# Latent attention scores from split operands, with the rotary parts stacked and the steps in another order

## The reference, cut to what matters

```python
c_q = rms_norm(h @ w_dq, cq_norm)
q = (c_q @ w_uq).reshape(b, s, MLA_HEADS, MLA_QK_NOPE + MLA_QK_ROPE)
q_nope = rms_norm(q[..., :MLA_QK_NOPE], q_nope_norm)
q_pe = rotary(rms_norm(q[..., MLA_QK_NOPE:], q_pe_norm), pos)
...
sc = (jnp.einsum('bqhd,bkhd->bhqk', qn, k_nope)
      + jnp.einsum('bqhr,bkr->bhqk', qp, k_pe)).astype(jnp.float32) * scale
sc = jnp.where(causal_mask(i, s), sc, NEG_INF)
a = jax.nn.softmax(sc, axis=-1)
return jnp.einsum('bhqk,bkhv->bqhv', a.astype(v.dtype), v)
```

## Time and profile before

| what | us |
|---|---|
| median of 3 runs | 2226.89 (2221.76 to 2227.26) |
| profiled execution | 2226.47 |
| its span, first to last instruction | 2224.7 |
| PE busy in the span | 2183.1 (98%) |
| DVE / ACT / POOL busy | 1276.9 (57%) / 945.7 (43%) / 804.4 (36%) |
| first scores of steps 1, 2, 3 | 763.40, 792.26, 824.28 |
| first scores of steps 7, 8 | 952.51, 984.93 |

### The profile page before, as it was taken

One profiled execution on the slowest core, in us unless ns is written; L12 is line 12 of the kernel. 1 busy time (PEld: TensorE's weight loads), 2 busy tenths in 40 slices (PEclk: granted clock), 3 DMA queues, 4 the chain that ended last, 5 costly groups with the idle time before them and its releaser, 6 DMA issues.

```text
span 2224.7 us, 25927 instructions
## 1 busy us (share of the span) xinstructions
PE 2183.1 (98%) x10008; PEld 1711.2 (77%) x10008; DVE 1276.9 (57%) x2198; ACT 945.7 (43%) x1558; POOL 804.4 (36%) x315
## 2 busy tenths in 40 slices
PE   8999999999999999999999999999999999999998
PEld 5777788888887767667888888887774688888887
DVE  6887665553258688773665562176967643333224
ACT  6676443333233566663344332233237532222224
POOL 1232444444443222113444444433330144444432
PEclk9999999999999999999999999999999999999999
...
DMA packets 58650, 199.97 MB, mean 90 GB/s; under 512 B 6720, under 2 KB 10320, under 8 KB 58528
## 3 DMA queue, kind: packets, MB, share of 16 engines
...
...
## 4 chain that ended last, share of the span: by engine, by line
PE 88%; DVE 7%; ACT 2%; issue 1%; DMA 1%; POOL 0%; SPq 0%; DVEq 0%; ACTq 0%
PE lin L535 24%; PE lin L537 24%; PE lin L536 24%; PE obank L869 1%; PE scores L847 1%; PE turn L668 1%; PE scores L851 1%; PE stat L674 1%; PE scores L1070 1%; PE lin L586 1%; PE obank L748 1%; PE lin L588 1%; PE lin L587 1%; PE scores L705 1%; PE obank L1046 1%
## 5 line engine op out<-in xcount | busy, mean ns | idle before, releaser
L2540 POOL TENSOR_TENSOR w_lo<-slots,w_hi 128x1024 fp32r<-128x1024 f32 (+4 forms) x309 | 801.5, 2596 | 1395.9 <-ACT w_hi L2021 1395.9
L2021 ACT ACTIVATE w_hi<-slots 128x1024 fp32r<-128x1024 f32 (+4 forms) x312 | 347.0, 1113 | 576.9 <-DMA slots<-in_w_ffn_in 281.0
L535 PE MATMUL lin<-g_hi,w_hi 128*128 128x512 f32 x1400 | 550.0, 393 | 0.0
L537 PE MATMUL lin<-g_hi,w_lo 128*128 128x512 f32 x1400 | 545.0, 389 | 0.0
L536 PE MATMUL lin<-g_lo,w_hi 128*128 128x512 f32 x1400 | 544.9, 389 | 0.0
L535 PEld LDWEIGHTS lin<-g_hi,w_hi 128*128 128x128 f32 x1400 | 262.8, 188 | 59.3 <-issue 5.0
L536 PEld LDWEIGHTS lin<-g_lo,w_hi 128*128 128x128 f32 x1400 | 262.8, 188 | 55.8 <-issue 1.7
L537 PEld LDWEIGHTS lin<-g_hi,w_lo 128*128 128x128 f32 x1400 | 262.7, 188 | 54.7
L1255 DVE TENSOR_TENSOR h<-lin,h 128x512 f32<-128x512 f32 x72 | 49.7, 690 | 306.1 <-PE lin L537 296.9
L536 PE MATMUL lin<-f_lo,w_hi 128*128 128x512 f32 x528 | 205.4, 389 | 0.0
L535 PE MATMUL lin<-f_hi,w_hi 128*128 128x512 f32 x528 | 205.4, 389 | 0.0
...
## 6 DMA issues: line engine op xcount, KB each, us to landing
...
slots<-in_w_b_pair SPq DMA_DIRECT2D x8, 768.0 KB, 4.2
...
```

Source lines behind the costliest of these rows:

```text
L535: pe.matmul(bank[:, parity, :], hi, x_hi, start=k == 0, stop=False)
L537: mm = pe.matmul(bank[:, parity, :], lo, x_hi, start=False, stop=k == len(rhs) - 1)
L2021: ac.activation(w_hi[:, slot, at_], slots[:, slot, at_], ACT.Copy).then_inc(q.hi_made, 1)
L2540: po.tensor_tensor(w_lo[:, slot, at_], slots[:, slot, at_], w_hi[:, slot, at_].bitcast(F32), ALU.subtract).then_inc(q.weights_split, 1)
```

## The change

Queries and keys are split into hi and lo parts of type fp32r. A head's scores are now five passes for each query block: q_hi·k_hi, q_hi·k_lo, q_lo·k_hi (L852 to L854 of the changed kernel), and two for the rotary part. For these, `b_qp[:, x]` stacks the hi and the lo part of head x's rotary query on the 128 partitions, against the hi part of the rotary key, which fills both halves, and its lo part (L855, L856). ScalarE makes the hi parts (`high_`, `rope_highs`, once `rope_key_high`), VectorE the lo parts (`low_`, `rope_lows`, once `rope_key_low`). Keys and stacked rotary queries have a single set of buffers, so their hi parts wait until all scores of the step are done; the scores of step s wait for all splits of step s-1 (`qk_split`). A reciprocal now serves both heads. The transposed weights of k = 3 go to a free third of the bank, so `turn_(3)` follows `turn_(2)` without a wait. `straight`, which was in `roped`, has a place of its own. The orders of all three engines' steps are new. Copies of the products out of PSUM (`output`) stay on VectorE.

```diff
@@ -130,6 +130,10 @@
...
+B_QK = 2 * AH + 1
+B_QK_ORDER = {0: 1, 1: 2, 3: 3, 4: 4, 2: 6}
...
@@ -294,11 +298,11 @@
...
-        b_kp = area(at, S); at += S
+        b_kp, b_kp_hi, b_kp_lo = area(at, S), area_r("b_kp_hi", 22 * S, S), area_r("b_kp_lo", at, S); at += S
...
-        b_qn = area(at, 2, 2, S); at += 4 * S
-        b_kn = area(at, 2, 2, S); at += 4 * S
-        b_qp = area(at, 2, S); at += 2 * S
+        b_q = [(area_r(f"b_q_hi{y}", o, 2, S), area_r(f"b_q_lo{y}", o + 2 * S, 2, S)) for y, o in enumerate((12 * S, at))]; at += 4 * S
+        b_k = area_r("b_k_hi", at, 2, S), area_r("b_k_lo", at + 2 * S, 2, S); at += 4 * S
+        b_qp = area_r("b_qp", at, 2, S); at += 2 * S
...
@@ -839,25 +843,27 @@
...
                         if k == 0:
-                            pe.wait_ge(q.b_normed, 5 * s)
-                            pe.wait_ge(q.b_rope, s)
-                        wait(pe, q.b_biased, 8 * (s - 1) + 2 * k)
-                        qb = slice(i * P, (i + 1) * P)
+                            pe.wait_ge(q.qk_split, B_QK + 6 * s)
+                        qb, keys = slice(i * P, (i + 1) * P), slice(0, LEN[i])
+                        (q_hi, q_lo), (k_hi, k_lo) = b_q[1 - par], b_k
                         for x in range(2):
-                            pe.matmul(scores[:, x, 0:LEN[i]], b_qn[:, 1 - par, x, qb], b_kn[:, 1 - par, x, 0:LEN[i]],
-                                      start=True, stop=False)
-                        for x in range(2):
-                            rows = slice(64 * x, 64 * x + 64)
-                            pe.matmul(scores[:, x, 0:LEN[i]], b_qp[rows, 1 - par, qb], b_kp[rows, 0:LEN[i]],
-                                      start=False, stop=True).then_inc(q.b_scored, 1)
+                            wait(pe, q.b_biased, 8 * (s - 1) + 2 * k - 1 + x)
+                            to = scores[:, x, keys]
+                            pe.matmul(to, q_hi[:, x, qb], k_hi[:, x, keys], start=True, stop=False)
+                            pe.matmul(to, q_hi[:, x, qb], k_lo[:, x, keys], start=False, stop=False)
+                            pe.matmul(to, q_lo[:, x, qb], k_hi[:, x, keys], start=False, stop=False)
+                            pe.matmul(to, b_qp[:, x, qb], b_kp_hi[:, keys], start=False, stop=False)
+                            pe.matmul(to, b_qp[:, x, qb], b_kp_lo[:, keys], start=False, stop=True).then_inc(q.b_scored, 1)
...
                         for x in range(2):
                             n, i = 8 * pair + 2 * k + x, NQ - 1 - k
                             pe.wait_ge(q.b_weights, n + 1)
-                            wait(pe, q.b_tcopied, n - 1)
-                            turn_weights(b_sc[:, x, i, :], i, turn[:, x, :]).then_inc(q.b_turned, 1)
+                            if k < 3:
+                                wait(pe, q.b_tcopied, n - 1)
+                            to = turn[:, x, 2 * P:] if k == 3 else turn[:, x, :]
+                            turn_weights(b_sc[:, x, i, :], i, to).then_inc(q.b_turned, 1)
...
 
                 if not proj and attn:
-                    early(0); turn_(2, s - 2, late); score(0); turn_(3, s - 2, late); product(0); score(1); product(1); early(1); score(2)
+                    early(0); turn_(2, s - 2, late); turn_(3, s - 2, late); score(0); product(0); score(1); product(1); early(1); score(2)
...
                 lin_(0)
                 if s == 1:
-                    rotated_(0); sums(4, 0)
-                lin_(1); turn_(2, s - 2, late); score(0); lin_(2); lin_(3); sums(0)
-                turn_(3, s - 2, late); score(1); lin_(4); sums(1); product(0); score(2); sums(2); lin_(5)
-                product(1); turn_(0); sums(3); lin_(6); score(3); rotated_(); sums(4); turn_(1)
+                    rotated_(0); sums(4, 0); lin_(1); lin_(2); score(0); lin_(3)
+                else:
+                    lin_(1); turn_(2, s - 2, late); turn_(3, s - 2, late); score(0); lin_(2); lin_(3)
+                sums(0); score(1); lin_(4); sums(1); product(0); sums(2); score(2); lin_(5)
+                product(1); turn_(0); sums(3); score(3); lin_(6); sums(4); rotated_(); turn_(1)
...
@@ -1657,17 +1664,18 @@
...
-                            ve.wait_ge(q.b_exped, n + 1)
-                            ve.reciprocal(d, d).then_inc(q.b_recip, 1)
-                            ve.wait_ge(q.b_recip, n + 1)
+                            if x == 0:
+                                both = den[:, 0:8].rearrange("p (x i) -> p x i", x=2)[:, :, i]
+                                ve.wait_ge(q.b_exped, n + 2)
+                                ve.reciprocal(both, both).then_inc(q.b_recip, 1)
+                                ve.wait_ge(q.b_recip, 4 * (s - 1) + k + 1)
                             ve.tensor_scalar(b_sc[:, x, i, 0:LEN[i]], b_sc[:, x, i, 0:LEN[i]], d, None, ALU.mult)\
                                 .then_inc(q.b_weights, 1)
...
                 def normed(j):
...
-                        dst = (b_qn[:, par, 0, :], b_qn[:, par, 1, :], b_rt[:, 0, :], b_kn[:, par, 0, :],
-                               b_kn[:, par, 1, :])[j]
+                        dst = b_rt[:, 0, :] if j == 2 else b_ri[:, j, :]
...
+                def low_(j):
+                    if proj:
+                        hi, lo = b_q[par] if j < 2 else b_k
+                        x = j % 2 if j < 2 else j - 3
+                        ve.wait_ge(q.qk_rounded, B_QK + 6 * s + B_QK_ORDER[j])
+                        ve.tensor_tensor(lo[:, x, :], b_ri[:, j, :], hi[:, x, :].bitcast(F32), ALU.subtract).then_inc(q.qk_split, 1)
+
+                def rope_lows():
+                    ve.wait_ge(q.qk_rounded, B_QK + 6 * s + 6)
+                    for x in range(2):
+                        rows, other = slice(64 * x, 64 * x + 64), slice(64 - 64 * x, 128 - 64 * x)
+                        ve.tensor_tensor(b_qp[other, x, :], b_rt[rows, 1, :], b_qp[rows, x, :].bitcast(F32), ALU.subtract)\
+                            .then_inc(q.qk_split, 1)
+
+                def rope_key_low():
+                    ve.wait_ge(q.qk_rounded, B_QK)
+                    ve.tensor_tensor(b_kp_lo[:, :], b_kp, b_kp_hi[:, :].bitcast(F32), ALU.subtract).then_inc(q.qk_split, 1)
...
+                def straight():
+                    ve.wait_ge(q.b_normed, 5 * s + 3)
+                    ve.tensor_tensor(b_rt[:, 2, :], b_rt[:, 0, :], cosb[:, :], ALU.mult).then_inc(q.b_terms, 1)
+
                 def roped():
                     ve.wait_ge(q.b_rotated, s + 2)
                     ve.tensor_tensor(b_rt[:, 1, :], obank[:, :], sinb[:, :], ALU.mult).then_inc(q.b_terms, 1)
-                    ve.tensor_tensor(b_rt[:, 2, :], b_rt[:, 0, :], cosb[:, :], ALU.mult).then_inc(q.b_terms, 1)
                     ve.wait_ge(q.b_terms, 3 + 2 * s + 2)
-                    ve.tensor_tensor(b_qp[:, par, :], b_rt[:, 1, :], b_rt[:, 2, :], ALU.add).then_inc(q.b_rope, 1)
+                    ve.tensor_tensor(b_rt[:, 1, :], b_rt[:, 1, :], b_rt[:, 2, :], ALU.add).then_inc(q.b_rope, 1)
...
                 if s == 0:
-                    take_(0); take_(1); square_split(0); take_(2); square_split(1); take_(3); square_split(2); normed(0)
-                    take_(4); square_split(3); normed(1); take_(5); square_split(4); normed(2); take_(6); normed(3)
-                    roped(); normed(4)
+                    take_(0); take_(1); square_split(0); rope_key_low(); take_(2); square_split(1); take_(3); square_split(2); normed(0)
+                    take_(4); square_split(3); normed(1); take_(5); square_split(4); normed(2); low_(0); take_(6); normed(3); low_(1)
+                    straight(); low_(3); roped(); normed(4); low_(4); rope_lows()
                     return
-                take_(0); take_(1); biased(0); square_split(0); take_(2); square_split(1); take_(3); weights_(0)
-                normed(0); biased(1); take_(4); square_split(2); first_half(0); output(0); first_half(1); biased(2)
-                square_split(3); normed(1); weights_(1); first_half(2, 3); take_(5); normed(2); output(1); square_split(4)
-                take_(6); first_half(4, 5); roped(); weights_(2); first_half(6, 7); biased(3); normed(3); normed(4)
-                weights_(3)
+                take_(0); square_split(0); take_(1); biased(0); square_split(1); take_(2); weights_(0)
+                take_(3); square_split(2); biased(1); normed(0); take_(4); square_split(3); normed(1); low_(0); output(0); first_half(0, 1)
+                biased(2); low_(1); weights_(1); first_half(2, 3); take_(5); square_split(4); normed(2); output(1); straight()
+                first_half(4, 5); biased(3); normed(3); take_(6); weights_(2); first_half(6, 7); low_(3); roped(); normed(4)
+                weights_(3); low_(4); rope_lows()
...
@@ -2293,12 +2322,32 @@
...
-                            ac.wait_ge(q.b_turned, 8 * pair + 2 * k + x + 1)
+                            ac.wait_ge(q.b_turned, 8 * pair + 2 * (3 if k > 1 else k) + x + 1)
                             if k == 0:
```

(35 more changed lines are left out.)

## The result

The changed kernel took 2259.99 us (median of 4 runs, 2255.34 to 2262.67), the kernel before 2226.69 on the same chip (4 runs): ratio 1.015, 95% interval 1.0136 to 1.0163. It is slower by 33 us, where 11 were forecast, and the time lies outside the range of 2217 to 2247. The direction and the place were right; two sizes and the clock were not. The nearest rival, the third (2246 us), fell short as well. Of a later kernel (e10) one execution of ten took 4398.88 us; it is left out of that kernel's ratio, and nothing here explains it.

A forecast was written before the change was run, and what follows sets the result against it. The prediction took VectorE, with ScalarE in its chain, as the new bound. Start +8.3, steps 2 to 6 +2.2, step 7 +2.8 and step 8 -1.6 gave 2226.5 + 11.7 = 2238.2 us, range 2217 to 2247.

The forecast's parts named there:

- TensorE alone: In a steady step, TensorE without waits for other engines would need 30.0 us, after savings of 1.5, 0.2 and 0.4.
- VectorE's work: In a steady step, VectorE's real work: 21.4 us before, plus 2.8 for subtractions less reciprocals, 24.2 us.
- The two GpSimd blocks: In each steady step, VectorE stands beside GpSimd's subtractions: 2.8 us at straight, 2.3 at normed(4), 5.1 in all.
- one of the signs named for being wrong: In the changed profile, the forecast is wrong if VectorE's long instructions are others than straight and normed(4), and shorter.
- VectorE's waits: In a steady step, VectorE's idle waits by the new order, with hand-overs, sum to 3.4 us.
- the layout: VectorE's steady step laid out by the new order, dense from normed(1) to the end: 32.5 us against 32.09.
- Rival 3: In steady steps, TensorE idle 2 to 3 us gets a lower clock: step 33.7, total 2246 us; chance 0.12.
- The start: Up to the first scores of step 2: lin_(2) of step 1 waits 4.6 us for take_(0); +8.3 us.
- Step 7: Step 7: 4.8 us more of output subtractions, 2.3 less for one GpSimd instruction; 35.2 instead of 32.42, +2.8.
- step 8: Step 8, without projection: TensorE bounds it and keeps the savings, -1.6 us.
- Rivals 1 and 2: The second: in steady steps one of the two GpSimd blocks falls on harmless instructions, step 31, total 2228 us; chance 0.24.
- rival 1: In steady steps TensorE stays the bound, GpSimd meeting PSUM copies and waits: 2211 us; chance 0.14 together with another rival.

The follow-up runs named there:

- e10: The kernel before, with both weight splits on ScalarE moved to the beginning of the step and square_split(0), (1) behind take_(2): 2222.82 us, ratio 0.9988.
- e3: The changed kernel with GpSimd's subtraction for these steps' weights cut to 32 columns, TensorE reading hi parts instead, passes unchanged: 2222.32 us in one run.
- e8: The changed kernel with both weight splits on ScalarE moved to the beginning of the step, square_split(0), (1) behind take_(2): 2219.9 us, ratio 0.9972.
- e2: The changed kernel with take_(5) moved behind square_split(4) and normed(2) in VectorE's order: 2246.05 us in one run.
- e1: The changed kernel with discarded products on TensorE ahead of score(0) and of lin_(2) of step 1: 2246.54 us in one run.

## Why the prediction was wrong

**TensorE alone, 30.0 a step: right.** e3 shows 29.86 and e8 30.15 (the 1.5 for `scores` mixes two ways of counting, see above; from start to start they went from 7.7 to 6.4, 1.3). Its passes of 512, 384 and 256 columns went every 0.23, 0.17 and 0.12 us, and of 128 columns every 0.11 (0.12 taken).

**VectorE's work, 24.2: right.** 29.22 less 2.66 and 2.15 of blocks is 24.4, and e8 has 24.43.

**The two GpSimd blocks, 5.1: right in size** (4.8), but the first was placed wrongly: `square_split(4)` stood, not `straight`, which is one of the signs named for being wrong.

**VectorE's waits, 3.4: the first term that was mis-sized.** They are 34.52 - 29.22 = 5.3 us at full clock. Each wait that the layout lists came within 0.3 us: 1.22 before `square_split(0)` (1.2 forecast), 0.23 and 0.66 before `take_(2)` and `weights_(0)` (0.5 and 0.5), 0.66 before `normed(1)` (0.7), 0.10 and 0.48 at the end (0.1 and 0.4). What is missing in it is one: the layout called the work from `normed(1)` on dense and overlooked that `take_(5)` writes `b_v`, and so waits for the last product that reads it. That is a wait of 1.71 us right before the block, so that the one follows the other instead of hiding it. e2 takes 1.2 of it away, and the step comes to an estimated 32.6 at full clock, the forecast's 32.5. This term is 5 x 2.0 = 10 us in steps 2 to 6.

**The clock: the second, and it was a rival instead of a term.** Rival 3 priced it at 1.2 a step from a clock of 0.96; measured are 1.2 to 1.35 us in three of five steps. It left out the start, where the 4.87 us wait is followed by `lin_(2)` and scores at the lower level. e1 gives the whole: 3.8 us up to the scores of step 2, 3.8 in steps 2 to 6, 1.1 in step 7. A forecast that has TensorE wait 2.5 us in each step and 4.6 once should have had the clock in its sum.

**The start, 8.3: right but for the clock.** Counted from `lin_(0)` of step 0, the scores of step 2 come 12.8 later than before, and 9.0 later in e1; from the first scores of step 1 to those of step 2 e1 has 29.79, where 29.8 was forecast. One reading on the way was wrong: the 19.02 in "25.66 - 19.02 = 6.6 us" is the column of TensorE's weight loads in the earlier trace rows. VectorE was busy 17.08 there and idle for 8.6, so that what had to fit fitted all the more.

**Step 7, 35.2: 37.5 at full clock (e1, from the first scores to the end of `rope_lows`) and 38.65 in the kernel itself.** The 4.8 us of output subtractions came as forecast. Of the 2.3 above it, 0.9 are a block: the forecast took 2.3 us off for one GpSimd instruction less, but two run in VectorE's way and cost 1.6 and 2.1. Another 1.0 is `normed(1)`, which waits 1.71 us for its factor, behind the roundings on ScalarE, instead of 0.7. The wait of `take_(5)` is not there.

**The tally** of 33.2 us of span against the sum of 11.7: the clock up to step 8 +8.8; steps 2 to 6 at full clock +10.2 (172.7 us in e1, 162.5 forecast); step 7 at full clock +2.3; the start +0.7; step 8 +0.2; ahead of step 0 +0.9 and behind the stage -1.7, where nothing was changed. Sum 21.4 of a difference of 21.5. The clock and the term of steps 2 to 6 thus make 19 of it, of about equal weight; the clock's size rests on a single execution.

Rivals 1 and 2, with GpSimd beside harmless instructions, did not happen here; e8 is what rival 1 described, 30.15 a step, once the work was put there on purpose.
